# A streaming encoder step on one core: second merge's inputs on ScalarE's queue, three reorderings, and a product's last three steps by tile

## What is computed

```
h = RMSNorm(x);  z = h @ w_in + b_in         # q,k,v of two branches, forget logits, two gates
A = sliding-window attention (sinks, bias);  B = forgetting attention (cached keys for the new tokens)
x = x + (sigmoid(ga) * (A @ w_oa) + sigmoid(gb) * (B @ w_ob)) @ w_out
x = x + SwiGLU(RMSNorm(x));  y = RMSNorm(x)
```

## Time and profile before

| | |
|---|---|
| median of 3 runs | 1594.77 us (1593.08 to 1595.02) |
| the profiled execution | 1592.57 us, its span 1590.8 us |
| PE, PEld busy | 1558.1, 1463.9 us (98%, 92%) |
| DVE, ACT, POOL busy | 1033.2, 702.0, 202.0 us |
| hardware DMA queue (SP) | 138.71 MB, 30.6% of 16 engines' span |
| software DMA queue (POOL) | 85.87 MB, 16.1% of 16 engines' span |

### The profile page before, as it was taken

One profiled execution on the slowest core, in us unless ns is written; L12 is line 12 of the kernel. 1 busy time (PEld: TensorE's weight loads), 2 busy tenths in 40 slices (PEclk: granted clock), 3 DMA queues, 4 the chain that ended last, 5 costly groups with the idle time before them and its releaser, 6 DMA issues.

```text
span 1590.8 us, 26537 instructions
## 1 busy us (share of the span) xinstructions
PE 1558.1 (98%) x10156; PEld 1463.9 (92%) x10156; DVE 1033.2 (65%) x2033; ACT 702.0 (44%) x1376; POOL 202.0 (13%) x356
## 2 busy tenths in 40 slices
PE   8999999999999999998999999999999999999997
PEld 8999999999999999977998999999999999888886
DVE  6655654566656654474674877766777777679864
ACT  6335555566656644352443642222322223434453
POOL 3012221110100110031010000000221122110000
PEclk9999999999999999999999999999999999999999
DMA  7153333434445355878464423322444445766442
GB/s 210 33 161 107 128 115 113 121 104 114 131 117 140 94 170 152 222 243 226 122 200 138 132 75 115 110 82 82 125 145 144 158 150 199 246 216 191 139 137 81
DMA packets 194348, 226.25 MB, mean 142 GB/s; under 512 B 23832, under 2 KB 145210, under 8 KB 193704
## 3 DMA queue, kind: packets, MB, share of 16 engines
q1 hardware_dynamic: 167840, 138.71, 30.6%
q0 software_dynamic: 26384, 85.87, 16.1%
HBM read 166.76 MB, written 57.82 MB: 141 GB/s over the span
## 4 chain that ended last, share of the span: by engine, by line
PE 85%; DVE 7%; DMA 3%; ACT 3%; issue 2%; SPq 0%; DVEq 0%; ACTq 0%; POOLq 0%
PE ps L2492 24%; PE ps L2493 24%; PE ps L2494 23%; PE ps L2558 3%; PE ps L2578 2%; DMA w_raw<-in_w_out_dram 2%; PE ps L2600 1%; PE ps L2601 1%; DVE sprob L1718 1%; PE ps L2615 1%; PE ps L2809 1%; PE ps L2808 1%; DMA w_raw<-in_w_ob_dram 1%; DVE e_lo L2134 1%; PE ps L2655 1%
## 5 line engine op out<-in xcount | busy, mean ns | idle before, releaser
L2492 PE MATMUL ps<-h_hi,w_hi 128*128 128x384 f32 (+1 forms) x816 | 274.1, 336 | 1.3 <-DVE h_lo L1690 1.2
L2494 PE MATMUL ps<-h_hi,w_lo 128*128 128x384 f32 (+1 forms) x816 | 266.5, 327 | 0.0
L2493 PE MATMUL ps<-h_lo,w_hi 128*128 128x384 f32 (+1 forms) x816 | 266.2, 326 | 0.0
L2492 PE MATMUL ps<-t_hi,e_hi 128*128 128x272 f32 x704 | 202.7, 288 | 0.9 <-DVE silu L2149 0.9
L2493 PE MATMUL ps<-t_lo,e_hi 128*128 128x272 f32 x704 | 202.8, 288 | 0.0
L2494 PE MATMUL ps<-t_hi,e_lo 128*128 128x272 f32 x704 | 202.1, 287 | 0.0
L2492 PEld LDWEIGHTS ps<-h_hi,w_hi 128*128 128x128 f32 x816 | 153.4, 188 | 3.4 <-DVE h_lo L1690 1.5
L2492 PE MATMUL ps<-b_hi,e_hi 128*128 128x272 f32 x528 | 152.5, 289 | 2.2 <-DVE silu L2149 1.1
L2493 PEld LDWEIGHTS ps<-h_lo,w_hi 128*128 128x128 f32 x816 | 153.5, 188 | 0.5 <-issue 0.5
L2494 PEld LDWEIGHTS ps<-h_hi,w_lo 128*128 128x128 f32 x816 | 153.2, 188 | 0.0
L2493 PE MATMUL ps<-b_lo,e_hi 128*128 128x272 f32 x528 | 152.1, 288 | 0.0
(11 more groups left out here) (372 smaller groups left out, 3631.2 us busy)
## 6 DMA issues: line engine op xcount, KB each, us to landing
w_raw<-in_w_gu_dram SPq DMA_DIRECT2D x104, 256.0 KB, 3.4
w_raw<-in_w_in_dram SPq DMA_DIRECT2D x68, 256.0 KB, 3.5
zg_d<-stg POOLq DMA_DIRECT2D x28, 544.0 KB, 3.0
act_d<-act POOLq DMA_DIRECT2D x44, 272.0 KB, 2.8
s_d<-s_sum POOLq DMA_DIRECT2D x44, 256.0 KB, 3.4
f_raw<-s_d SPq DMA_DIRECT2D x44, 256.0 KB, 3.0
f_raw<-act_d SPq DMA_DIRECT2D x33, 256.0 KB, 2.7
w_raw<-in_w_out_dram SPq DMA_DIRECT2D x32, 256.0 KB, 3.6
```

The lines of the kernel that those rows point to most:

```text
L2492: nc.tensor.matmul(out, l_hi, r_hi, start=start, stop=False)
L2493: nc.tensor.matmul(out, l_hi, r_lo, start=False, stop=False)
L2494: return nc.tensor.matmul(out, l_lo, r_hi, start=False, stop=stop)
```

## The change

Five edits. (1) `THREE_TO` falls by two units, and the four quarters of the first cached key block are turned at steps 128, 130, 132, 134; with it the turn of the first inverse sums moves from step 129 to 127. (2) In the last new-token unit (s == 3) VectorE normalises before it splits branch A's inputs of group 0 and scales branch B's four before it subtracts branch A's; ScalarE casts them earlier, between the dense evacuations. (3) Group 0's first product waits for one dense evacuation fewer. (4) Group 1's merge inputs are issued by ScalarE, in four portions behind the gates' sigmoid of blocks 1 to 4 of `merge(0)`, instead of by POOL behind all of group 0's gates. (5) For product P2 the last three steps go tile by tile, instead of two.

```diff
-THREE_FROM, THREE_TO = N_SWA, N_SWA + 56
+THREE_FROM, THREE_TO = N_SWA, N_SWA + 54
...
+def last_steps(i):
+
+    return 3 if F_ORDER[i] == "P2" else 2
...
-            turns_at[(130, 132, 133, 134)[c]].append(("cache", 0, c))
+            turns_at[(128, 130, 132, 134)[c]].append(("cache", 0, c))
...
-            load_outputs(pool, 1, 0)
-            pool.wait_ge(sem("ab_lo"), 8)
-            load_sums(pool, 1, 0)
             load_gates(1, 0)
-            for slot in range(2):
-                pool.wait_ge(sem(f"abs_saved{slot}"), 64 * 2)
-            pool.wait_ge(sem("ab_scaled"), 8)
-            load_outputs(pool, 1, 1)
-            load_sums(pool, 1, 1)
-            for x in range(2):
-                pool.dma_start(rooms[1]["ab_b"][:, x, :, 512:576].bitcast(F32), ots_d[x]).then_inc(sem("ab_landed11"), 16)
             load_gates(1, 1)
...
                 if s < 3:
                     turned_hi(("cache", s + 1, 2))
+                else:
+                    for k in range(2, 4):
+                        merged_in_hi(0, 0, k)
                 evac(d + 1)
                 if s < 3:
                     turned_hi(("cache", s + 1, 3))
                     stage_hi(("new", s + 1))
                 else:
-                    for k in range(2, 4):
-                        merged_in_hi(0, 0, k)
+                    for k in range(4):
+                        merged_in_hi(0, 1, k)
                 evac(d + 2)
                 turned_hi(("ots", s))
-                if s == 3:
-                    for k in range(4):
-                        merged_in_hi(0, 1, k)
...
+            def second_inputs(k):
+
+                if k == 0:
+                    a.wait_ge(o_ready, N_DUOS + 4)
+                    load_outputs(a, 1, 0)
+                elif k == 1:
+                    a.wait_ge(sem("ab_lo"), 8)
+                    load_sums(a, 1, 0)
+                elif k == 2:
+                    for slot in range(2):
+                        a.wait_ge(sem(f"zg_saved{slot}"), 16 * saves(NB - 2 + slot))
+                        a.wait_ge(sem(f"abs_saved{slot}"), 64 * 2)
+                    a.wait_ge(sem("ab_scaled"), 8)
+                    load_outputs(a, 1, 1)
+                else:
+                    load_sums(a, 1, 1)
+                    for x in range(2):
+                        a.dma_start(rooms[1]["ab_b"][:, x, :, 512:576].bitcast(F32), ots_d[x]).then_inc(sem("ab_landed11"), 16)
...
                     if j + 1 < KD:
                         gates(j + 1)
+                    if g == 0 and 1 <= j < 5:
+                        second_inputs(j - 1)
...
                     merged_in_scale(0, 0, (2, 3))
+                normalise(N_STREAM + s)
+                if s == 3:
+                    merged_in_scale(0, 1, (0, 1, 2, 3))
                     for k in range(4):
                         merged_in_lo(0, 0, k)
-                normalise(N_STREAM + s)
...
                 turned_lo(("ots", s))
                 if s == 3:
-                    merged_in_scale(0, 1, (0, 1, 2, 3))
                     for k in range(4):
                         merged_in_lo(0, 1, k)
...
-                        pe.wait_ge(*((z_evac, N_DENSE) if k < 2 else (part_done, n_pieces)))
+                        pe.wait_ge(*((z_evac, N_DENSE - 1 + k) if k < 2 else (part_done, n_pieces)))
...
-                    for k in range(NK - 2):
+                    for k in range(NK - last_steps(i)):
...
-                    n = NK * i + NK - 2
-                    tiles = tile_order(i)
+                    tiles, n = tile_order(i), NK * i + NK - last_steps(i)
                     for t in tiles:
-                        for x in range(2):
+                        for x in range(last_steps(i)):
...
-                            elif x == 1:
+                            elif x == last_steps(i) - 1:
                                 last.then_inc(sem("tile_done"), 1)
```

## The result

The changed kernel takes 1596.08 us (median of 20 runs, 1593.58 to 1601.24), the kernel before in the same session 1594.48 (20 runs, 1592.35 to 1596.14): ratio 1.0013, 95% interval 1.0007 to 1.0019. That is 0.1% slower, where 1590.3 was forecast. The profiled spans stand further apart, 1594.2 against 1590.8, since the profiled run of the kernel before was 1.9 us under its median and the other one at its own. One of the ten runs of the kernel before that stand beside the last four experiments was slow (1703.54 us) and is left out of their median.

The account below looks back on a forecast made before the run. TensorE, busy 98% of the span, was taken as the bound, leaving pauses, low clock and the end. Terms -1.2 - 2.4 - 7.7 + 6.9 - 0.1 + 1.6 + 1.1 - 2.7 gave -4.5, so 1590.3 us, range 1583 to 1601.

Parts of the forecast that it names:

- +6.9 for block 5: First merge: x and the gate wait behind group 1's inputs, so block 5 begins at 708.5, a wait of 6.9 us.
- Weights starve: Rival, first merge: weight chunks' small packets wait behind other queues, 12 to 22 us per chunk; 1602.6 us, chance 0.24.
- Clock: TensorE's low clock: +1.6 us behind the new pause in the merge, -3.1 us as it goes from the output product.
- Later blocks: First merge after block 5: weights still share with the third and fourth portion, +1.1 us (0 to 13).
- The output product: Its pauses and low clock go once inputs land earlier: 4.1 + 0.5 + 3.1, so -7.7 us.
- Keys: Turns of cached keys, two steps apart: the 1.34 us wait for VectorE goes, taken as -1.2 us.
- Start: First merge's start: VectorE's reordered scalings let the subtractions of `ab_b` start earlier, -2.4 us.
- End: Last steps of P2: the new tokens' tile is finished 12 products earlier and all tiles follow, -2.7 us.
- a sum of +3.2: Whole kernel by the skill's page alone: the new queue is worth nothing, the -7.7 is struck out, 1598.0 us.

Follow-up runs that it names:

- the last four experiments: Small-chunk rows of 2 KB without edit 4, 1586.88 us; the change with portions two blocks later, 1587.37, or at deadlines, 1580.71; deadline-paced POOL loads, first portion behind gate 7, 1584.92.
- without the new queue: The change with its fourth edit undone, so POOL issues group 1's inputs in its old order: 1587.1 us, ratio 0.9957.
- start and end alone: Two runs on the kernel before: only the second and third edits, 1590.81 us; only the fifth edit, 1591.22 us.
- the paced pair: The change with group 1's inputs issued by deadline and its first two gates held back: from POOL, without edit 4, 1580.44 us; from ScalarE, 1580.71 us.
- POOL's early version: The change, but POOL issues group 1's inputs, as early as the change does, with no queue of ScalarE's: 1600.09 us, ratio 1.0032.
- ScalarE's paced version: The change with its four portions issued from ScalarE at blocks 5 and 6 and two output-product chunks, group 1's first two gates held back: 1580.71 us, ratio 0.992.
- the paced version: The change without its fourth edit, POOL's loads of group 1's inputs paced by their deadlines, group 1's first two gates held back: 1580.44 us, ratio 0.9909.
- the new queue alone: The kernel before with the fourth edit alone, so ScalarE issues group 1's inputs: 1602.36 us, ratio 1.0051.

## Why the prediction was wrong

**The step that failed** is the +6.9 for block 5. Its mechanism was to be the gate: x and the gate behind it wait for 32 to 40 packets of inputs, gate at 702.9 to 704.2, then sigmoid, two issues, cast and subtraction. The gate did land at 704.5, and by the estimate above it alone would have made a pause of 6.7. But the text took it for granted that the weight chunk would be there. It landed at 713.9 and set block 5: 716.29 instead of 708.5. The pause was 14.63, not 6.9, 7.7 us more.

The rival "Weights starve" had the mechanism and nearly the size, 12 to 22 us per chunk, where 23.2 were found. With a quarter of the packets the chunk took 11.6 us and was no longer waited for. I gave the rival 0.24 and argued against it that the chunk of the earlier trace rows had not stopped TensorE. Yet at 10.7 us it was already what ScalarE waited for last, by 0.51 us. A chunk at its limit beside one other queue should have been the first thing to reprice beside two. The rule of the packets was in the earlier trace rows, and I used it for the large packets only. With the third queue the small ones got 47 turns per us instead of 95.

The rival's own sum was 6.5 us too high. It let block 6 start at 729, when nearly all inputs had arrived; it started at 724.38. SP had issued its chunk 4 us behind block 5's and both landed within 4 us of each other, while ScalarE issued the fourth portion only from 713.95 on. One long pause paid for both. That the third portion would come late stood among my reasons against the rival, and there it was right.

**Clock** (+1.6 in the merge, -3.1 in the output product): the loss in the merge was 2.4, in the output product 2.8 went. **Later blocks**, +1.1: measured 0.40. **The output product**: its pauses are gone and it runs at 24 products in 5.45 us, as said. The gain there was real. (The 14.3 us named for the chunk ahead of that product are its second DMA's; the earlier trace rows has 12.5, the middle of the two.)

**Keys** (-1.2): the 1.34 us wait of the earlier trace rows has no successor among the pauses. It was not timed alone; without the new queue the edits give 7.2, start and end alone 3.6 and 3.2; the 0.4 that is left is less than such a difference can tell. **Start** (-2.4): in the trace yb(0) is 3.65 earlier, 2.31 of them with the start's edits alone, so 1.34 may be the keys'. **End**: -2.7 by the trace, to the tenth.

So the sum of -4.5 became +3.4 in the spans: of the 7.9 between them one term makes 7.7, and the others nearly cancel (clock +0.8, output product +0.3, later blocks -0.7). In the medians it is +1.6; two traces of kernels that are the same up to there differed by 2.7 at the second merge, so the tenths of such a sum say little.

The text had weighed, and put aside, what the Trainium skill says ("DMA: Bandwidth & Descriptors", section "Issuing engines are not separate DMA queues"), that another issuer only saves issue time. By it I had a sum of +3.2, 1598.0, closer than mine. That is luck: this sum struck out the -7.7 of the output product, which came (4.6 of pauses, 2.8 of clock), and kept the waits of the merge, which the same rule would have struck out too; -1.2 - 2.4 - 2.7 were then left. The paced pair agrees with the page (1580.44 in POOL's queue, 1580.71 in ScalarE's). What the sum by it had left out: a queue of its own makes the issue early, and early was the harm.

**Where the expected gain went**: it was given back ahead of where it was earned. By the earlier trace rows the engines had 5.3 us free from 685 to 715. The inputs need 21, by the earlier trace rows. The change put them where x's 2 MB already were. The difference, 15.7, is near the 15.0 us of pauses that came, but this is no proof: the fourth portion was issued from 713.95 on, when the chunk that ended the pause had landed. The output product, with a share of 0.31 when left alone, had the room.

**What stays open.** Why the start alone gave 3.6 rather than 2.3 us. Why the chunk's first packets came 4 to 5 us behind its issue, in the kernel before and in the change. Why two DMA issues kept ScalarE for 5 to 6 us in two of the runs and for 1.3 in others. And in POOL's early version no run parts the effect of the order within the queue from that of the burst at 715 to 719 us.

## What to carry to other kernels

Before moving a load, list who else has work queued in that stretch, by queue and in packets. Here queues with work took turns packet by packet, so the one with 512-byte rows got 10.5% of the engines' time beside two with rows of 2 KB and more, and it carried the loads with the tightest cover. Then give each load a deadline and place it where the DMA share is low, one portion between two chunks that are due (7.3 to 10.7 us for the chunk) and not two (13.4 us). Which engine issues it mattered little at the right moment; at a bad one two issues kept ScalarE from its next cast for 5.9 us. A load that is on time by half a microsecond is the first to reprice, whatever the change aims at. And where a wait ends with TensorE's `w_lo`, look one engine further back: the same kind of pause was ended by a weight chunk, by a gate or by a DMA issue.

## What the runs showed that I had not expected

- Three queues share as strictly as two: 190, 190 and 189 packets in 4 us. The rate of turns is not set by the number of queues alone: 95 per queue and us in the earlier trace rows, 47 with three queues, but with two queues in POOL's early version 98 in one microsecond and 46 in the next. What sets it was not parted.
- A full set of DMA engines (share 1.07 over 15 us) need not cost TensorE anything: the weight chunks issued from 728 to 741 us in ScalarE's paced version landed within 9.6 us. The same share with a chunk of 23.2 us stood beside a pause of 14.6 us.
- In the changed kernel the granted clock fell to 0.50 at 704.6, 2.9 us after TensorE stopped, and came back some 5.3 us after it had begun again. Behind the pause of 2.13 us in the paced version it stayed at 1.00; with the new queue alone it fell 1.2 us after a pause of 1.95 (10 products in 3.60 us), so the length of the pause alone does not tell.
- A quarter of the packets (2-KB rows) brought the chunk's landing from 23.2 to 11.6 us, but only a third of the pauses went: behind the chunk stood the gate, and behind the gate ScalarE's own DMA issues.
